# Cross attention: value weights as the moving operand with 512 columns, softmax steps issued two deep

## The reference, cut to what matters

```python
def memory_cross_attention(xn, memn, wq, w_kv, wo):
    B, S, _ = xn.shape                                  # 1, 512
    q = (xn @ wq).astype(jnp.float32).reshape(B, S, XATTN_HEADS, XATTN_HEAD_DIM)
    kv = (memn @ w_kv).astype(jnp.float32).reshape(B, MEM_LEN, 2, XATTN_HEADS, XATTN_HEAD_DIM)
    s = jnp.einsum('bshc,bmhc->bhsm', q, kv[:, :, 0]) * (XATTN_HEAD_DIM ** -0.5)
    p = jax.nn.softmax(s, axis=-1)
    o = jnp.einsum('bhsm,bmhc->bshc', p, kv[:, :, 1]).reshape(B, S, D_MODEL)
    return (o @ wo.astype(jnp.float32)).astype(xn.dtype)
```

## Time and profile before

| | |
|---|---|
| median of 3 runs | 3152.41 us (3146.73 to 3152.45) |
| profiled execution, its own time | 3146.47 us |
| its span | 3144.6 us |
| mean granted TensorE clock | 0.941 |
| TensorE busy | 2830.1 us, 90% of the span |
| cross attention, value units of the two passes | 2568.2 to 2589.7 us and 2658.9 to 2680.5 us |
| cross attention, softmax stretches | 2589.7 to 2623.8 us and 2680.5 to 2713.3 us |

### The profile page before, as it was taken

The page is one execution under the profiler, slowest core; times in us unless marked ns, Lnnn a source line. Parts: engine busy times, 40 slices in busy tenths (PEclk is TensorE's granted clock), DMA queues, the critical chain, the costliest instruction groups (busy, mean ns, idle before and its releaser), DMA issues.

```text
span 3144.6 us, 44003 instructions
## 1 busy us (share of the span) xinstructions
PE 2830.1 (90%) x17517; PEld 2057.1 (65%) x17517; DVE 1629.2 (52%) x2182; ACT 649.0 (21%) x1101; POOL 178.0 (6%) x203
## 2 busy tenths in 40 slices
PE   5799668899989989999799999979889988889998
PEld 3455443688878868888355655565567776668886
DVE  6677672544445554444455555542355463365554
ACT  3133311211011021110222222222221121121101
POOL 2000110000000000000111110000000000000000
PEclk8899768999999999999899999999789989999999
DMA  7376201333332323333111111112023332223332
GB/s 229 116 238 198 70 0 47 89 91 100 92 88 87 94 80 93 94 94 95 49 30 30 31 30 31 32 55 66 24 59 93 87 85 62 60 75 98 96 93 67
DMA packets 404222, 255.33 MB, mean 81 GB/s; under 512 B 19880, under 2 KB 389121, under 8 KB 403969
## 3 DMA queue, kind: packets, MB, share of 16 engines
q1 hardware_dynamic: 400496, 243.63, 26.6%
q0 software_dynamic: 2320, 5.11, 0.5%
q10 hardware_dynamic: 1280, 4.78, 0.4%
HBM read 250.60 MB, written 2.10 MB: 80 GB/s over the span
## 4 chain that ended last, share of the span: by engine, by line
PE 84%; DVE 9%; issue 3%; ACT 3%; DMA 1%; DVEq 0%; ACTq 0%; POOL 0%; SPq 0%; POOLq 0%
PE PS L722 13%; PE PS L723 13%; PE PS L724 13%; PE PS L1398 5%; PE PS L709 4%; PE PS L737 3%; PE PS L738 3%; PE PS L739 3%; PE PS L1373 3%; PE PS L1150 3%; PE PS L1461 1%; PE PS L1379 1%; PE PS L1487 1%; PE PS L1583 1%; PE PS L1485 1%
## 5 line engine op out<-in xcount | busy, mean ns | idle before, releaser
L748 DVE CAST WH<-W 128x1024 fp32r<-128x1024 f32 x304 | 210.9, 694 | 719.0 <-PE PS L724 547.8
L750 DVE TENSOR_TENSOR WL<-W,WH 128x1024 fp32r<-128x1024 f32 x304 | 372.5, 1225 | 10.4
L723 PE MATMUL PS<-XNL,WH 128*128 128x512 f32 x864 | 342.8, 397 | 0.0
L722 PE MATMUL PS<-XNH,WH 128*128 128x512 f32 x704 | 277.1, 394 | 0.0
L724 PE MATMUL PS<-XNH,WL 128*128 128x512 f32 x704 | 275.3, 391 | 0.0
L724 PE MATMUL PS<-HH,WL 128*128 128x512 f32 x672 | 261.5, 389 | 0.0
L722 PE MATMUL PS<-HH,WH 128*128 128x512 f32 x672 | 261.5, 389 | 0.0
L723 PE MATMUL PS<-HL,WH 128*128 128x512 f32 x672 | 261.5, 389 | 0.0
L737 PE MATMUL PS<-XNH,WH 128*128 128x512 f32 x448 | 180.3, 402 | 32.6 <-DVE XNL L681 32.5
L738 PE MATMUL PS<-XNL,WH 128*128 128x512 f32 x480 | 193.9, 404 | 0.0
L1398 PE MATMUL PS<-HXF,W 128*128 128x512 f32 x336 | 167.5, 625 | 22.4 <-DVE ARENA L2549 11.5
(11 more groups left out here) (467 smaller groups left out, 4812.9 us busy)
## 6 DMA issues: line engine op xcount, KB each, us to landing
ARENA<-in_ada_w SPq DMA_DIRECT2D x80, 512.0 KB, 5.1
W<-in_ffn_w SPq DMA_DIRECT2D x64, 512.0 KB, 3.9
W<-in_w_in SPq DMA_DIRECT2D x51, 512.0 KB, 4.1
W<-in_ffn_w_gate SPq DMA_DIRECT2D x44, 512.0 KB, 3.8
W<-in_ffn_w_up SPq DMA_DIRECT2D x44, 512.0 KB, 3.7
W<-in_ffn_w_down SPq DMA_DIRECT2D x32, 512.0 KB, 3.8
W<-in_sc_w_in SPq DMA_DIRECT2D x24, 512.0 KB, 3.7
W<-in_ada_w SPq DMA_DIRECT2D x16, 512.0 KB, 4.9
```

Of the source, the lines that this page charges most:

```text
L722: nc.tensor.matmul(dst, WH[:, h, c], hi(k), start=(start and k == 0), stop=False)
L723: nc.tensor.matmul(dst, WH[:, h, c], lo(k), start=False, stop=False)
L748: nc.vector.tensor_copy(WH[:, h, :], W[:, s, 0:D]).then_inc(parted, 1)
L750: nc.vector.tensor_tensor(WL[:, h, :], W[:, s, 0:D], WH[:, h, :], ALU.subtract).then_inc(freed[s], 1)
```

## The change

Three things change in each pass of cross attention; nothing else in the program does.

1. Units 8 to 11 no longer hold 128 value columns by all 1024 weight rows, but 512 columns by 256 rows. The DMA moves as many bytes, in pieces of 2 KB where they were 512 B. A value matmul has 512 moving columns. All four units add into banks 0 and 1 (one for each half of the memory), and V is complete only after unit 11.
2. ScalarE copies V in two copies of 128x512 after unit 11, where it made four of 128x256, one after each unit. TensorE's scores no longer wait for V's copy.
3. The softmax steps stand one deeper on each engine: TensorE `s0 s1 s2 t0 s3 t1 ...`, ScalarE `exp0 exp1 t0 exp2 t1 ...`, VectorE `max0 max1 inv0 p0 max2 inv1 p1 ...`. No buffer is added: `SX`, the score banks and the transpose banks are two each, as before.

```diff
-        xa_act = prog("xa_act", "q0 q1 q2 q3 v0 v1 v2 v3 " + " ".join(f"exp{s} t{s}" + ...
+        xa_act = prog("xa_act", "q0 q1 q2 q3 v0 v1 exp0 " + " ".join((f"exp{s + 1} " if s < 7 else "") + f"t{s}" + ...
-        xa_dve = prog("xa_dve", "k0 k1 k2 k3 " + " ".join(f"max{s} inv{s} p{s}" + ...
+        xa_dve = prog("xa_dve", "k0 k1 k2 k3 max0 " + " ".join((f"max{s + 1} " if s < 7 else "") + f"inv{s} p{s}" + ...
-        xa_pe = prog("xa_pe", "s0 " + " ".join((f"s{s + 1} " if s < 7 else "") + f"t{s}" + (" pv0" if s == 4 else "") ...
+        xa_pe = prog("xa_pe", "s0 s1 " + " ".join((f"s{s + 2} " if s < 6 else "") + f"t{s}" + (" pv0" if s == 4 else "") ...
@@ SyncE
-                    nc.sync.dma_start(tiles(s), w_cols(src, i * (4 * P) + (u % 4 * P + (D if u >= 8 else 0)))).then_inc(landed[s], 16)
+                    if u < 8:
+                        nc.sync.dma_start(tiles(s), w_cols(src, i * (4 * P) + u % 4 * P)).then_inc(landed[s], 16)
+                    else:
+                        rows = slice(2 * (u - 8), 2 * (u - 8) + 2)
+                        nc.sync.dma_start(tiles(s, 2, 4 * P), w_cols(src, i * (4 * P) + D, 4 * P)[:, rows, :]).then_inc(landed[s], 16)
@@ TensorE
-                        pe.wait_ge(xa_act.sem, xa_act.done(f"q{u - 8}", i))
+                        if u == 8:
+                            pe.wait_ge(xa_act.sem, xa_act.done("q1", i))
                         for c in range(NC):
-                            dst, t = bank[u - 8][:, c * P:(c + 1) * P], slice(c * P, (c + 1) * P)
-                            for k in range(KD):
-                                w = slice(k * P, (k + 1) * P)
-                                nc.tensor.matmul(dst, MNH[:, k, t], WH[:, h, w], start=(k == 0), stop=False)
-                                nc.tensor.matmul(dst, MNH[:, k, t], WL[:, h, w], start=False, stop=False)
-                                mm = nc.tensor.matmul(dst, MNL[:, k, t], WH[:, h, w], start=False, stop=(k == KD - 1))
+                            t = slice(c * P, (c + 1) * P)
+                            for n in range(2):
+                                k, w = 2 * (u - 8) + n, slice(n * 4 * P, (n + 1) * 4 * P)
+                                nc.tensor.matmul(bank[c], MNH[:, k, t], WH[:, h, w], start=(k == 0), stop=False)
+                                nc.tensor.matmul(bank[c], MNH[:, k, t], WL[:, h, w], start=False, stop=False)
+                                mm = nc.tensor.matmul(bank[c], MNL[:, k, t], WH[:, h, w], start=False, stop=(k == KD - 1))
-                pe.wait_ge(xa_act.sem, xa_act.done("v3", i))
...
@@ ScalarE
-                for u in range(4):
-                    act.wait_ge(multiplied, splits.used("xa", 8 + u, i))
-                    nc.scalar.activation(VX[:, :, u * P:(u + 1) * P], bank[u][:, 0:TC]..., ACT.Copy)...
+                act.wait_ge(multiplied, splits.used("xa", 11, i))
+                for c in range(NC):
+                    nc.scalar.activation(VX[:, c, :], bank[c], ACT.Copy)...
```

More of the change, by code:

```diff
@@ L535, in two_blocks @@
         norm_x2 = NormStage(prog, "norm_x2", False, parts=True, early=True)
-        xa_act = prog("xa_act", "q0 q1 q2 q3 v0 v1 v2 v3 " + " ".join(f"exp{s} t{s}" + {5: " o0", 7: " o1"}.get(s, "") for s in range(8)), loop=True)
-        xa_dve = prog("xa_dve", "k0 k1 k2 k3 " + " ".join(f"max{s} inv{s} p{s}" + {5: " o0", 7: " o1"}.get(s, "") for s in range(8)), loop=True)
-        xa_pe = prog("xa_pe", "s0 " + " ".join((f"s{s + 1} " if s < 7 else "") + f"t{s}" + (" pv0" if s == 4 else "") for s in range(8)) + " pv1", loop=True)
+        ended_head = {5: " o0", 7: " o1"}
+        xa_act = prog("xa_act", "q0 q1 q2 q3 v0 v1 exp0 " + " ".join((f"exp{s + 1} " if s < 7 else "") + f"t{s}" + ended_head.get(s, "") for s in range(8)), loop=True)
+        xa_dve = prog("xa_dve", "k0 k1 k2 k3 max0 " + " ".join((f"max{s + 1} " if s < 7 else "") + f"inv{s} p{s}" + ended_head.get(s, "") for s in range(8)), loop=True)
+        xa_pe = prog("xa_pe", "s0 s1 " + " ".join((f"s{s + 2} " if s < 6 else "") + f"t{s}" + (" pv0" if s == 4 else "") for s in range(8)) + " pv1", loop=True)
         norm_ffn2 = NormStage(prog, "norm_ffn2", False, parts=True, early=True)
@@ L1716, in _ @@
                 scores(0)
+                scores(1)
                 for s in range(8):
-                    if s < 7:
-                        scores(s + 1)
+                    if s < 6:
+                        scores(s + 2)
                     turn(s)
@@ L2076, in _, with exps @@
                     nc.scalar.activation(QX[:, u, :], bank[u], ACT.Copy, scale=(2 * P) ** -0.5).then_inc(xa_act.sem, xa_act.step(f"q{u}"))
-                for u in range(4):
-                    act.wait_ge(multiplied, splits.used("xa", 8 + u, i))
-                    nc.scalar.activation(VX[:, :, u * P:(u + 1) * P], bank[u][:, 0:TC].rearrange("p (c d) -> p c d", c=NC), ACT.Copy).then_inc(xa_act.sem, xa_act.step(f"v{u}"))
-                for s in range(8):
-                    e, qt = divmod(s, 4)
+                act.wait_ge(multiplied, splits.used("xa", 11, i))
+                for c in range(NC):
+                    nc.scalar.activation(VX[:, c, :], bank[c], ACT.Copy).then_inc(xa_act.sem, xa_act.step(f"v{c}"))
+                def exps(s):
                     act.wait_ge(xa_dve.sem, xa_dve.done(f"max{s}", i))
@@ L2086, in _ @@
                                                      accum_out=ROWSUM2[:, s:s + 1]).then_inc(xa_act.sem, xa_act.step(f"exp{s}"))
+                exps(0)
+                for s in range(8):
+                    e, qt = divmod(s, 4)
+                    if s < 7:
+                        exps(s + 1)
                     act.wait_ge(xa_pe.sem, xa_pe.done(f"t{s}", i))
@@ L2710, in _, with row_max @@
                         nc.vector.tensor_copy(KX[:, u - 4, :], bank[u][:, 0:TC]).then_inc(xa_dve.sem, xa_dve.step(f"k{u - 4}"))
-                for s in range(8):
+                def row_max(s):
                     dve.wait_ge(xa_pe.sem, xa_pe.done(f"s{s}", i))
                     nc.vector.tensor_reduce(NEGMAX2[:, s:s + 1], bank[4 + s % 2][:, 0:TC], AXX, ALU.max, negate=True).then_inc(xa_dve.sem, xa_dve.step(f"max{s}"))
+                row_max(0)
+                for s in range(8):
+                    if s < 7:
+                        row_max(s + 1)
                     dve.wait_ge(xa_act.sem, xa_act.done(f"exp{s}", i))
```

## The result

| | before | after |
|---|---|---|
| median | 3152.43 us (4 runs, 3146.73 to 3157.60) | 3115.77 us (4 runs, 3110.15 to 3128.22) |
| profiled execution, its own time | 3146.47 us | 3128.22 us |
| its span, mean granted clock | 3144.6 us, 0.941 | 3126.4 us, 0.938 |

The ratio is 0.9891 with a 95% interval of 0.9865 to 0.9916: faster, by 26 to 43 us. Forecast were 3118 us and a gain of 31.4 us; the medians differ by 36.7 us.

What follows compares the result with a forecast made beforehand. TensorE alone was taken as the limit in the value units, the chain from engine to engine in the softmax stretches. Gains of 21.0 + 10.4 = 31.4 us, taken off the runs of before, gave 3118 us, range 3108 to 3129.

Steps and rivals of the forecast that it cites:

- Value units: Value matmuls in cross attention: 0.227 us each at 512 columns, 10.9 us a pass instead of 21.4, 21.0 gained in both.
- What could be late: In the shorter value units: VectorE's split, with 0.6 us left, and the weights, with 3.6 us left, stay in time.
- Copies of V: Two wide copies on ScalarE ahead of `exp0`: cost 0, hidden by the split; without that cover up to 1.2 us a pass.
- Steps 0 to 4: First softmax steps: 1.17 us a step instead of 2.04, first transposes 0.27 us later, 3.2 us gained a pass.
- Steps 5 to 7: Last softmax steps: `pv1` 2.8 us after the subtraction instead of 5.0, a gain of 2.2 us a pass.
- Sum: Both passes of cross attention: 21.0 us from value units and 10.4 from softmax, 31.4 us gained, giving 3118 us.
- Clock: TensorE's granted clock falling before `pv1`: costed at 0, with 2 us in each pass kept on either side.
- The deep order pays: Softmax steps: against the forecast's 10.4 us gain stood a rival that the deeper order brings nothing, 3128.5 us, chance 10%.
- the clock did not stay up: Rival at `pv1`: shorter idling no longer lets the clock fall, 2 to 3 us more a pass, 3112 us, chance 7%.
- The two remaining rivals: Value matmuls: wide costs four narrow, 0.446 us, 3139 us, chance 2%; or is taken in two passes, 3179 us, 1%.
- The loop of two steps: Softmax steps: `exp`, scores two steps on, transposes' copy, next `exp` close a loop of 2.33 us for two steps.

Runs made afterwards that it cites:

- e1: The kernel before with only the wide value units and their V copies, softmax order as before: median 3126.0 us, ratio to before 0.9908.
- e5: The change with 256 moving columns in the value matmuls, 24 for a unit instead of 12: 3127.6 us in one run.
- e4: The change with head 0's copy and subtraction moved from behind step 5 to behind step 7: medians 3112.3 and 3107.3 us, and one run of 3102.5.
- e2: The kernel before with only the deeper softmax order on all three engines, value units and V copies as before: median 3135.4 us, ratio to before 0.9955.
- e6: e4 plus matmuls whose result nobody reads in TensorE's idle places around `pv1`: median 3099.6 us, ratio to before 0.9842; 3106.6 in one later run.
- e3: The change with TensorE's softmax order put back, ScalarE and VectorE still two deep: median 3129.4 us, ratio to before 0.9926.
- e7: e4 with only ScalarE two deep, TensorE and VectorE in the order of before: 3106.9 us in one run.

## Why the prediction was right, point by point

- **Value units.** 0.227 us a matmul from rows of another stage with as many columns; measured 0.227. 10.9 us a pass, as forecast. e1 shows the part alone: 21.3 against 21.0 us. Why four narrow ones cost about two wide ones was left open there; e5 shows a floor of some 0.11 us a matmul, with 256 columns at 0.120; what sets the floor is not shown.
- **What could be late.** Neither the split (VectorE waits for TensorE up to 0.8 us, where 0.6 of room was reckoned) nor the weights (landed in 3.6 us).
- **Copies of V.** Cost 0, as forecast.
- **Steps 0 to 4.** 1.18 us a step against 1.17. TensorE alone was reckoned at 1.08 us and needs 1.14, so the figure lies close above TensorE's own limit and would have come out nearly as well with a somewhat shorter loop. The first transposes came 4.33 us behind the last value matmul instead of 3.84, 0.5 late where 0.27 was reckoned; transposes(0) to `pv0` took 4.96 us (2595.48 to 2600.44).
- **Steps 5 to 7.** From the maximum of step 7 (2607.90) to `pv1` (2610.79) 2.89 us against 2.8. From transposes(5) to `pv1` the prediction has 5.8 us; its own gain of 2.2 us gives 5.95, and 6.05 were measured.
- **Sum.** Both passes without the product between them: 55.6 to 39.3 and 54.4 to 38.7 us, 32.0 against 31.4. The product between the passes took 36.5 instead of 35.1 us, since the clock stayed at the low level for an estimated 5.8 us of it where it was 3.0. That is inside the 2 us a pass kept on either side.
- **Clock, and luck.** Cost 0 came out because the clock was low in as much of the stretch after the change as before, an estimated 20.5 us each. That is luck: three profiles of the one kernel of e4 have 13.7, 6.8 and 3.7 us. That 3118 lies 2.2 us from the median of 3115.8 is partly luck too, since the four runs spread over 18 us and the medians' gain of 36.7 us is 6 us more than the stretches show.
- **Rivals.** The deep order pays (e2); the clock did not stay up (`pv1` 5.95 and 5.61 us). e6 shows one way to keep it up. The two remaining rivals are excluded by the pace and by one record a matmul.
- **A right number with a gap in its reason.** The loop of two steps holds with all three orders changed, but the prediction left VectorE's queue out of it: the text before had the maximum only as "hidden". e3 shows a second loop through that queue, which makes the steps slower than before (2.35 us) unless the scores stand ahead on TensorE.

## What to carry to other kernels

Take the price of a matmul in a new width from the distance of starts of a dense stream of that width and type. For the fp32r matmuls here, each with its own weight load, 128 and 256 columns cost nearly the same and 512 nearly twice as much, so up to 256 the number of matmuls counts. When a chain over several engines is to be issued deeper, draw the loop through every queue, in-order neighbours included, for each engine's order apart: with TensorE's order alone left behind, the steps were slower than with none changed. Look at what else stands in the queue at the end of such a chain; moving one head's copy and subtraction brought 6.9 to 11.5 us here, 6.3 of them by the waits.

## What the runs showed of the hardware

- A fp32r matmul with its weight load costs 0.112 us at 128 moving columns, 0.120 at 256 and 0.227 at 512, at the full clock. The Trainium skill, "TensorE: Matmul & The Clock Gate", section "LDWEIGHTS (loading the stationary operand)", gives columns divided by 1.2 as the nanoseconds of a weight load. For 128 columns that is an estimated 107 ns. The 0.112 us seen here lie close to it, but the trace's rows of weight loads are 0.192 us long, and no run here has a matmul without a weight load that could tell the two apart.
- The clock fell around TensorE's idle places: in e4 during `pv1` and, in the first pass, again at the next product, in e7 in the second step of a pass. With the idle places from transposes(5) to the next product filled, it fell nowhere in the stretch, in both profiles.
- The time before cross attention is not fixed: in 13 profiles, with the same work up to there, the first value matmul started between 2562.3 and 2581.1 us, and in three profiles of one kernel (e4) at 2565.1, 2567.3 and 2574.3. That is much of the scatter of the whole runs; a change of 10 us is read more surely from its own stretch than from medians of four.
